# Prompt attention two heads at a time, with matmuls on alternating halves of the array

## The reference, cut to what matters

```
def sparse_attend(q, k_sel, v_sel, sel, q_pos, valid, rel_bias):
    logits = jnp.einsum('bthd,btkhd->bthk', q, k_sel).astype(jnp.float32) * HEAD_DIM ** -0.5
    bias = rel_bias[t5_bucket(sel - q_pos[None, :, None])]
    logits = logits + jnp.moveaxis(bias, -1, -2).astype(jnp.float32)
    logits = jnp.where(valid[:, :, None, :], logits, -jnp.inf)
    p = jax.nn.softmax(logits, axis=-1).astype(v_sel.dtype)
    return jnp.einsum('bthk,btkhd->bthd', p, v_sel)
```

## Time and profile before

| | us |
|---|---|
| median of 3 runs | 2533.11 |
| lowest and highest | 2530.53, 2541.93 |
| span of the profiled execution | 2543.9 |
| the attention stage in it, from its first matmul to its last vector instruction | 771.5 to 1022.6 |
| waiting for its tables before that | 757 to 771.5 |

### The profile page before, as it was taken

The page is one execution under the profiler, slowest core; times in us unless marked ns, Lnnn a source line. Parts: engine busy times, 40 slices in busy tenths (PEclk is TensorE's granted clock), DMA queues, the critical chain, the costliest instruction groups (busy, mean ns, idle before and its releaser), DMA issues. The chain is left out here.

```text
span 2543.9 us, 32792 instructions
## 1 busy us (share of the span) xinstructions
PE 2243.4 (88%) x13085; PEld 2029.4 (80%) x13085; DVE 1364.6 (54%) x2010; ACT 683.0 (27%) x922; POOL 495.5 (19%) x303
## 2 busy tenths in 40 slices
PE   4999999926658999788796999999999999999994
PEld 3879999924445676468575999999999999999993
DVE  5579999886523475224253454444454434444556
ACT  3222112212133344201332322222232222222222
POOL 0111122162100000111202222222222222222223
PEclk9999999967775699789898999999999999999996
DMA  4102323210021000333421111111111111111114
GB/s 114 45 25 84 95 83 84 75 51 13 10 62 42 1 1 1 134 108 100 141 73 52 49 44 48 43 50 43 50 43 48 44 43 50 43 50 43 42 34 147
DMA packets 180905, 146.77 MB, mean 58 GB/s; under 512 B 27563, under 2 KB 157067, under 8 KB 180755
## 3 DMA queue, kind: packets, MB, share of 16 engines
q1 hardware_dynamic: 179482, 140.50, 18.3%
q0 software_dynamic: 1280, 4.20, 0.5%
HBM read 117.94 MB, written 25.82 MB: 57 GB/s over the span
## 5 line engine op out<-in xcount | busy, mean ns | idle before, releaser
L57 PE MATMUL ps<-g_xT_h,f_wh 128*128 128x344 f32 x1536 | 327.8, 322 | 17.2 <-POOL f_wl L2025 11.4
L57 PE MATMUL ps<-g_xT_l,f_wh 128*128 128x344 f32 x1536 | 326.8, 321 | 0.0
L2025 POOL TENSOR_TENSOR f_wl<-f_wst,f_wh 128x1024 fp32r<-128x1024 f32 x96 | 248.7, 2591 | 396.8 <-ACT f_wh L2072 396.8
L57 PE MATMUL ps<-g_xT_h,f_wl 128*128 128x344 f32 x1536 | 325.2, 320 | 0.0
L57 PEld LDWEIGHTS ps<-g_xT_h,f_wh 128*128 128x128 f32 x1536 | 259.2, 189 | 19.0 <-POOL f_wl L2025 11.5
L2163 DVE TENSOR_TENSOR g_fT<-ps,g_fT 128x1032 f32<-128x1032 f32 x128 | 157.5, 1230 | 211.7 <-PE ps L57 211.7
L57 PEld LDWEIGHTS ps<-g_xT_l,f_wh 128*128 128x128 f32 x1536 | 260.8, 189 | 0.0
L57 PEld LDWEIGHTS ps<-g_xT_h,f_wl 128*128 128x128 f32 x1536 | 256.7, 188 | 0.0
L2138 DVE COPY f_acc<-g_conv 128x8 f32 (+1 forms) x64 | 35.5, 555 | 375.9 <-ACT f_acc L2086 375.9
L2082 ACT ACTIVATE f_up<-ps 128x1032 f32<-128x1032 f32 x64 | 66.3, 1035 | 451.4 <-PE ps L57 451.4
L481 PE MATMUL ps<-g_hT_h,j_wh 128*128 128x344 f32 (+1 forms) x840 | 182.9, 326 | 0.2 <-POOL j_wl L318 0.2
(11 more groups left out here) (394 smaller groups left out, 3546.5 us busy)
## 6 DMA issues: line engine op xcount, KB each, us to landing
f_wst<-in_w_up SPq DMA_DIRECT2D x64, 512.0 KB, 4.1
j_wst<-in_w_in SPq DMA_DIRECT2D x34, 512.0 KB, 4.3
f_wst<-in_w_down SPq DMA_DIRECT2D x32, 512.0 KB, 3.5
d_gates<-j_ring SPq DMA_DIRECT2D x16, 516.0 KB, 3.0
m_gt<-d_gates SPq DMA_DIRECT2D x16, 516.0 KB, 4.8
n_x<-in_x_prompt SPq DMA_DIRECT2D x8, 512.0 KB, 6.6
a_v<-in_cache_v POOLq DMA_DIRECT2D x16, 256.0 KB, 7.1
a_k<-in_cache_k SPq DMA_DIRECT2D x16, 256.0 KB, 2.9
```

What stands on the lines that cost most here:

```text
L57: mm = pe.matmul(ps[0:m, 3 * slot + c, 0:CH], w[:, k, 0:m], x[:, k, c * CH:(c + 1) * CH], start=(first and k == 0 and n == 0), stop=(last ...
L2025: pool.tensor_tensor(wl[:, s, :], wst[:, s, :], wh[:, s, :].bitcast(F32), ALU.subtract).then_inc(w_lo, 1)
```

## The change

A step is now a query block and a pair of heads (2m, 2m+1), 32 steps. `scores` walks the chunks and issues, for each, the even head's product (rows 0 to 63) and then the odd head's (rows 64 to 127), into two PSUM regions; then both heads' bias tables. `weigh` alternates in the same way between the two heads for each key block: output partitions 0 to 63, then 64 to 127. `turn`, `pt_copy`, `logits`, `probs` and `scale` stay single, e being the head within the pair. `pt` has four buffers instead of two. The orders of the engines are rewritten:

```
-                if n >= 2:
-                    pe.wait_ge(l_done, n - 1)
+                if n:
+                    pe.wait_ge(l_done, 2 * n)
                 for c in range(0, w, BANK):
+                    k = min(BANK, w - c)
+                    for e in range(2):
+                        r = e * HD
+                        pe.matmul(psf[:, e * 1024 + c:e * 1024 + c + k], g.qT[r:r + HD, m, i * P:(i + 1) * P],
+                                  g.kT[r:r + HD, m, c:c + k], start=True, stop=False, skip_group_check=True)
...
             def weigh(n):
+                i, m = pairs[n]
+                pe.wait_ge(pt_done, 2 * n + 2)
...
+                if n >= 2:
+                    pe.wait_ge(yl_done, n - 1)
                 for j in range(i + 1):
+                    for e in range(2):
+                        r = e * HD
+                        mm = pe.matmul(ps[r:r + HD, 6 + n % 2, 0:P], vv[:, j, (2 * m + e) * HD:(2 * m + e + 1) * HD],
+                                       pt[:, buf(n, e), j * P:(j + 1) * P], start=(j == 0), stop=(j == i),
+                                       skip_group_check=True)
                 mm.then_inc(y_done, 1)
...
+            for n in range(NPAIR + 2):
+                if n < NPAIR:
                     scores(n)
+                if 1 <= n <= NPAIR:
+                    turn(n - 1, 0)
+                if n >= 2:
+                    weigh(n - 2)
+                if 1 <= n <= NPAIR:
+                    turn(n - 1, 1)
```

ScalarE:

```
+            for n in range(NPAIR + 2):
+                if 1 <= n <= NPAIR:
+                    pt_copy(n - 1, 0)
+                if n < NPAIR:
+                    probs(n, 0)
+                if n >= 2:
+                    y_high(n - 2)
+                if n < NPAIR:
+                    probs(n, 1)
+                if 1 <= n <= NPAIR:
+                    pt_copy(n - 1, 1)
```

VectorE:

```
+            for n in range(NPAIR + 2):
+                if n < NPAIR:
+                    logits(n, 0)
+                if 1 <= n <= NPAIR:
+                    scale(n - 1, 1)
+                if n < NPAIR:
+                    logits(n, 1)
+                    scale(n, 0)
+                if n >= 2:
+                    y_low(n - 2)
+                k = n - (NPAIR - 4 - LATE_ROUNDS)
+                if 0 <= k < LATE_ROUNDS:
+                    late_round(k)
```

More of the change, by code:

```diff
@@ L1265, in phase_attention, with buf @@
         block = ctx.enter_context(nc.Block())
-        steps = [(i, h) for i in range(NT) for h in range(H)]
-        NSTEP = len(steps)
+        pairs = [(i, m) for i in range(NT) for m in range(H // 2)]
+        NPAIR = len(pairs)
+        def buf(n, e):
+            return (n % 2) * 2 + e
         masks = [mask01[:, 0:P], mask01[:, P:3 * P]] + list(g.mask)
@@ L1292, in _, with probs, pt_copy @@
             act.activation(t8h[:, :, :], t8[:, :, :], ACT.Copy).then_inc(th_done, 1)
[L1294 to L1302, removed]
+            def probs(n, e):
+                w = (pairs[n][0] + 1) * P
+                act.wait_ge(nmx_done, 2 * n + e + 1)
+                act.activation(lg[:, buf(n, e), 0:w], lg[:, buf(n, e), 0:w], ACT.Exp, bias=nmx[:, 2 * n + e:2 * n + e + 1],
+                               accum_out=den[:, 2 * n + e:2 * n + e + 1]).then_inc(e_done, 1)
+            def pt_copy(n, e):
+                w = (pairs[n][0] + 1) * P
+                act.wait_ge(turned, 2 * n + e + 1)
                 if n >= 2:
                     act.wait_ge(y_done, n - 1)
-                act.activation(pt[:, n % 2, 0:w], psf[:, 4 * BANK:4 * BANK + w], ACT.Copy).then_inc(pt_done, 1)
+                act.activation(pt[:, buf(n, e), 0:w], psf[:, 4 * BANK:4 * BANK + w], ACT.Copy).then_inc(pt_done, 1)
             def y_high(n):
-                i, h = steps[n]
+                i, m = pairs[n]
                 act.wait_ge(y_done, n + 1)
[L1310 to L1319, removed]
+                act.activation(g.ya_h[:, m, i * P:(i + 1) * P], ps[:, 6 + n % 2, 0:P], ACT.Copy).then_inc(yh_done, 1)
+            for n in range(NPAIR + 2):
[9 more added lines that the diff above has]
+                    pt_copy(n - 1, 1)
         @block.vector
@@ L1332, in _, with logits @@
             dve.tensor_tensor(t8l[:, :, :], t8[:, :, :], t8h[:, :, :].bitcast(F32), ALU.subtract).then_inc(tl_done, 1)
-            def logits(n):
-                i = steps[n][0]
+            def logits(n, e):
+                i, c = pairs[n][0], 2 * n + e
                 w = (i + 1) * P
[L1337 to L1340, removed]
+                dve.wait_ge(s_done, c + 1)
+                if n >= 2:
+                    dve.wait_ge(turned, c - 3)
+                dve.tensor_tensor_reduce(out=lg[:, buf(n, e), 0:w], in0=psf[:, e * 1024:e * 1024 + w],
@@ L1341, in logits @@
                                          in1=masks[i], scale=0.125, scalar=-3.0e38, op0=ALU.add, op1=ALU.max,
[L1342 to L1351, removed]
+                                         accum_out=mx[:, c:c + 1]).then_inc(l_done, 1)
@@ new lines, in logits, with scale @@
+                dve.wait_ge(l_done, c + 1)
+                dve.tensor_scalar(nmx[:, c:c + 1], mx[:, c:c + 1], -1.0, None, ALU.mult).then_inc(nmx_done, 1)
+            def scale(n, e):
+                w, c = (pairs[n][0] + 1) * P, 2 * n + e
+                dve.wait_ge(e_done, c + 1)
+                dve.reciprocal(rden[:, c:c + 1], den[:, c:c + 1]).then_inc(r_done, 1)
+                dve.wait_ge(r_done, c + 1)
+                dve.tensor_scalar(lg[:, buf(n, e), 0:w], lg[:, buf(n, e), 0:w], rden[:, c:c + 1], None,
@@ L1352, in scale @@
                                   ALU.mult).then_inc(p_done, 1)
             def y_low(n):
[L1355 to L1358, removed]
+                i, m = pairs[n]
+                dve.wait_ge(yh_done, n + 1)
+                o = g.ya_h[:, m, i * P:(i + 1) * P]
+                dve.tensor_tensor(g.ya_l[:, m, i * P:(i + 1) * P], ps[:, 6 + n % 2, 0:P], o.bitcast(F32),
```

62 lines of the change are left out of this document (19 added, 43 removed).

## The result

| | before | after |
|---|---|---|
| median | 2531.82 us | 2455.1 us |
| lowest and highest | 2530.09, 2541.93 (4 runs) | 2451.5, 2459.74 (4 runs) |
| ratio | | 0.9695, 95% interval 0.9666 to 0.9725 |
| span of the profiled execution | 2543.9 us | 2452.2 us |
| attention phase, first to last instruction | 265.7 us | 178.7 us |

Of the 91.7 us between the two profiled executions 87 lie in the attention phase. (The phase is all of `phase_attention`, with its wait for the tables; the stage is the part of it from the first logits on.)

The account below looks back on a forecast made before the run. TensorE was taken to bound every block; blocks 0 to 3 minus 26 us, 4 to 6 minus 14, 7 minus 14.2, sum -54, taken as 53 for small waits. Median from 2533.1 to 2480 us, range 2463 to 2506.

Parts of the forecast that it names:

- TensorE bounds every block before: All query blocks of the kernel before: TensorE sets the pace, so work taken off it shortens the stage.
- the division of a head's time: Block 7 before, one head: scores 1.91 us, tables 0.34, transposes 0.96, value products 1.90; 5.11 in all.
- Both halves run at once: Scores and value products of a pair: two halves in the time of one, minus 1.72 and 1.74 us in block 7.
- Rival 1: Scores: the row halves don't overlap, so the saving is half, minus 34 us, 2499; chance 0.13.
- rival 2: Scores and value products: strict program order, one slot more than half per pair, minus 42 us, 2491; chance 0.08.
- The pair of block 7 and the tight wait: Block 7: pair 10.22 to about 6.5 us, block 32.3; TensorE's wait for both logits before scores holds by 0.3.
- VectorE binds blocks 4 to 6: Blocks 4 to 6: VectorE's 75.4 us of work becomes the bound; 82.4 us against 96.3, minus 14.
- The clock: Block 3: the clock rises with the same block of work as before, at about 855; blocks 0 to 3 take 81 us.
- rival 3: Block 2: clock rises earlier, about 815, through fewer changes of use a pair; minus 70 us, 2463; chance 0.06.
- The base: Profiled execution of 2543.9 us; its distance from the median has no tie to the stage, so median 2533.1 becomes 2480.
- The slower rival: Whole stage: clock stays at half as TensorE has too little to do; 2540 us; chance 0.06, half slower by over 0.5%.
- Rival 5: Whole stage at half clock: blocks 4 to 7 take 172 us against 142.9, net plus 4 to 7, 2540; chance 0.06.

Follow-up runs that it names:

- six changes: Changed kernel with both heads on one half of the array, scores and tables issued head by head, six changes of use a pair: 2521.64 us, ratio 0.9959.
- the two kernels with the long blocks first: Changed and ungrouped kernels, query blocks 3 to 7 first, then 2, 1, 0, late rounds beside pairs 3 to 14, twelve products ahead: 2455.05 us and 2509.46 us.
- one half: Changed kernel with both heads of a pair on the same half of the array, so no overlap, result not attention: 2504.34 us, ratio 0.9895.
- the run with the scores in a row: Changed kernel with only the scores' alternation undone, even head's scores then odd head's, value products still alternating: 2460.8 us, ratio 0.9719.
- ungrouped: Changed kernel's buffers and pairs, but TensorE goes head by head on opposite halves, `y_high` at the end of ScalarE's turn: 2539.68 us, ratio 0.9999.
- the added products: Twelve fp32 products on TensorE during its wait for the tables; added to the kernel before 2534.79 us (1.0004), to the changed kernel 2456.13 us (0.9709).
- the version without them: Changed kernel, long query blocks first, three late rounds in VectorE's wait for the tables, no added products: 2454.52 us (0.9681); with them 2450.06 us (0.9649).

## Why the prediction was wrong, step by step

**TensorE bounds every block before: right**, and so was the division of a head's time. Removing work from it removed time in every block.

**Both halves run at once: right.** Value products as read from the earlier trace rows, scores by the same reading, both at full overlap. Rival 1 (scores don't overlap) and rival 2 (strict order) are out.

**The pair of block 7 and the tight wait: right.** 6.38 for 6.5 a pair, 32.36 for 32.3 the block. The reserve at the single set of score regions held.

**VectorE binds blocks 4 to 6: right, the size a little off.** I allowed 5 us for its waits and 2 for a late clock. It had 2.6 of idle time over the three blocks and no late clock, and its own work took 74.2 for 75.4: 76.8 for 82.4.

**The clock: this step failed.** I took the rise to come with the same block of work as before, at about 855. It came at 791.30:

```profile
770.10:791.20 21.10, 20.25 (x89) 12.91 (x88) 12.34 (x71) 9.51 (x41) 0.00 (x0) 0.50 0.10 23
791.30:933.00 141.70, 122.88 (x1106) 86.88 (x1106) 118.19 (x319) 87.30 (x183) 0.00 (x0) 1.00 0.01 1
```

That makes blocks 0 to 3 27 us shorter than forecast, and it is the whole difference but for the 5.6 of blocks 4 to 6 and some 5 us outside the phase and at the borders, where the profiled executions differ too. My rival 3 had the direction, but gave as its reason fewer changes of use a pair, placed the rise at 815 and got a chance of 0.06; "six changes" shows that their number isn't the reason. I argued that the rise goes with the block, since blocks 1 and 2 of before had no gap and stayed low. The runs show that it goes with how TensorE's work is grouped: in the old block order it comes 15 to 32 us after the first logits in nine profiles with two heads' value products in one stretch, and 55 to 94 us in four head by head.

**The base: this failed too, the other way.** I worked from a profiled execution with a stage of 250 us, and wrote that its distance from the median has no tie to this stage. The second one had 232.5, and 17.4 of the 19.5 us between the two lie in the stage, so there is a tie. The runs of the kernel before spread from 2521 to 2551 us. The changed kernel spreads from 2451 to 2465, with the rise in block 1 in both its profiles. By the profiled executions the gain is 91.7 us, by the medians 77. Had I known the rise at 791, my sum would have been 53 + 27 + 6 = 86, against 77. The chance that one sample of a moment that varies is a late one belonged into the range.

**How the 77 us divide.** At equal clock the new pattern is worth 55.5 us, near the 53 to 54 of my sum, which was in effect one for a clock that doesn't change. That the two are so close is in part luck. From first logits to first logits of the blocks, the two kernels with the long blocks first differ by 21 us in blocks 0 to 3, 19 in blocks 4 to 6 and 15 in block 7, where I had 26, 14 and 14: the first was reckoned at half clock, where the same work costs more, and the second with waits that VectorE didn't have. The other 20 or so of the 77 are the clock's; this is what is left over, and no run measured it by itself. By the other route: the order alone, with no overlap, gave 26 us (0.9895), and the overlap 51 (0.9695 against 0.9895). Of the 26 the clock is the larger part: the phase of "one half" (226.4 us) is 39 and 21 us shorter than in the two profiles of before, and the rise, 66 and 28 us earlier at half the pace, accounts for 33 and 14 of that.

**The slower rival** (the clock stays low) did not happen; the fear that overlapped streams leave TensorE with too little was the wrong way round. Without overlap it rose after 27 and 32 us, in the seven profiles with overlap and the old block order after 15 to 22. One echo of it is there: in two of these seven the clock was down again for a few us in block 7, which made the block 1.7 us longer. In the second profile of the changed kernel:

```profile
905.00:909.60 4.60, 2.92 (x38) 2.44 (x39) 4.43 (x11) 2.35 (x5) 0.00 (x0) 1.00 0.00 0
909.80:913.00 3.20, 3.20 (x9) 0.84 (x5) 0.80 (x2) 1.82 (x3) 0.00 (x0) 0.50 0.01 3
```

TensorE pauses for 1.5 us at the same place, at the start of block 7, in both profiles of the changed kernel, and only one of them has the dip. The other dip, in the run with the scores in a row, comes 1 us after a pause of 1.95; the first profile of the changed kernel has one of 1.94 there and stays at 1.00.

**Small slips.** ScalarE is busy up to 45% of a block, not 44, and VectorE down to 31% (block 2), less than a third. The clock drops at 753.8, 3.4 us before the phase's first instruction at 757.2, and not while TensorE waits for its tables. Rival 5's own terms, 172 less 142.9 less 26, give plus 3 and not plus 4 to 7. None of these moves the forecast.

**What stays open.** Why the grouped stretches raise the clock sooner, and which part of the order does it. "Six changes" and "ungrouped" differ in the grouping of the value products, in whether transposes and value products stand between the two heads' scores, in the halves that the heads use and in the place of `y_high`, and I did not separate them. The rise in "six changes" is from one profile, and the moments vary. What lowers the clock after the added products is open too. Why these lengthen the feed-forward phase was not tried: beside the version without them, the profile with them shows six more pauses of TensorE in it, of 0.6 to 0.9 us, some 142 us apart.

## What to carry to other kernels

Where heads of 64 channels take turns on TensorE, put two side by side on opposite halves of the array, in the rows for the scores and in the output for the value products: streams that were the bound took half the time here (1.90 us for 32 value products), and the next engine (here VectorE with its late rounds) became the bound. Look in the trace for a place where such instructions happen to meet; one boundary at the end of a stage was enough to size the value products, and the scores followed them. In a stage that is partly at half clock, look at the rise in more than one profiled execution before using it in a sum, and count on it moving when the order of the work changes.

## What the runs showed of the hardware

- TensorE ran matmuls on another half of the array ahead of three earlier ones in the program: 4 + 4 score instructions in a row took 1.99 us like alternating ones, 16 + 16 value products 3.33 us against 1.97 alternating and 3.71 on one half. The Trainium skill (TensorE: Matmul & The Clock Gate, "The mechanism") says that matmuls start and end in program order; these runs show otherwise for fp32.
- TensorE without idle time ran at 1.2 GHz for 85.20 us. It had fallen there from 2.4 GHz within 2 us of the first logits, after a pause of 2.04 us; short steps of blocks 1 and 0 with no such pause ran at 2.4 GHz for 29 us in another kernel.
- The moment of the rise differed by 38 us between two executions of the same kernel, and its stage by 17 us.
- With twelve matmul calls added in one phase, another phase, 500 us later, was 6 us longer (1147.8 us against 1141.6); the cause is not known.
